# Latent attention: the softmax probabilities are normalised on ScalarE instead of VectorE

## The reference

```python
def blocked_attention(q, k, v, scale):
    ...
    def one_block(qblk):
        s = jnp.einsum('bqhgd,bkhd->bhgqk', qblk, k).astype(jnp.float32) * scale
        p = jax.nn.softmax(s, axis=-1).astype(v.dtype)
        return jnp.einsum('bhgqk,bkhd->bqhgd', p, v)
    ...

def mla_attend(q_nope, q_rope, ckv, k_rope, w_kv_b):
    B, T, _ = ckv.shape
    kv = (ckv @ w_kv_b).reshape(B, T, MLA_HEADS, QK_NOPE + V_DIM)
    k = jnp.concatenate([kv[..., :QK_NOPE],
                         jnp.broadcast_to(k_rope[:, :, None, :], (B, T, MLA_HEADS, QK_ROPE))], axis=-1)
    q = jnp.concatenate([q_nope, q_rope], axis=-1)[:, :, :, None]
    return blocked_attention(q, k, kv[..., QK_NOPE:], (QK_NOPE + QK_ROPE) ** -0.5)
```

## Time and profile before

| | us |
|---|---|
| median of 3 runs | 1293.79 (1293.59 to 1293.82) |
| the profiled execution, its own time | 1294.56 |
| its span, first to last instruction | 1292.7 |
| PE busy | 1262.9 (98% of the span) |
| DVE busy | 827.4 (64%) |
| ACT busy | 532.3 (41%) |
| latent-attention stage (first to last exponential of L1540) | 976.4 to 1155.3 |

### The profile page before, as it was taken

How to read it: one execution, slowest core, us unless ns; L and a number is a source line. 1 busy time by engine, 2 the same in 40 slices (tenths; PEclk the granted TensorE clock), 3 DMA queues, 4 the chain that set the end, 5 groups by cost and what they waited for, 6 DMA issues and landing times.

```text
span 1292.7 us, 17320 instructions
## 1 busy us (share of the span) xinstructions
PE 1262.9 (98%) x6691; PEld 1050.3 (81%) x6691; DVE 827.4 (64%) x1257; ACT 532.3 (41%) x967; POOL 58.2 (5%) x80
## 2 busy tenths in 40 slices
PE   5999999999999999999999999999999999999997
PEld 2556677788888878888887788999989999988885
DVE  3344756775667757675874767987386666664445
ACT  4234343354333333344334544333365554543333
POOL 0000300000100010000000200000000000000000
PEclk9999999999999999999999999999999999999999
DMA  9999788445666457644885467675332222226443
GB/s 388 399 417 392 281 303 284 141 145 178 222 217 228 126 191 238 203 159 155 284 297 168 146 216 242 213 240 170 120 99 79 68 65 66 66 65 247 154 151 134
DMA packets 65521, 257.17 MB, mean 199 GB/s; under 512 B 7992, under 2 KB 8120, under 8 KB 60320
## 3 DMA queue, kind: packets, MB, share of 16 engines
q1 hardware_dynamic: 59616, 234.96, 52.5%
q0 software_dynamic: 5536, 20.52, 4.9%
q10 hardware_dynamic: 288, 0.59, 0.1%
HBM read 248.10 MB, written 7.93 MB: 198 GB/s over the span
## 4 chain that ended last, share of the span: by engine, by line
PE 94%; DMA 2%; DVE 2%; issue 1%; ACT 1%; SPq 0%; POOL 0%; ACTq 0%; POOLq 0%
PE gemm L560 18%; PE gemm L562 17%; PE gemm L561 17%; PE turned L717 3%; PE gemm L758 3%; PE gemm L760 3%; PE gemm L759 3%; PE gemm L532 2%; PE gemm L534 2%; PE gemm L533 2%; PE attended L799 2%; PE ada_bank L696 2%; PE ada_bank L640 1%; DMA w_raw<-in_w_all 1%; PE scores L717 1%; DMA ada<-in_ada_first 1%
## 5 line engine op out<-in xcount | busy, mean ns | idle before, releaser
L1637 DVE TENSOR_TENSOR w_lo<-w_raw,w_hi 128x1024 fp32r<-128x1024 f32 x241 | 296.9, 1235 | 265.6 <-ACT w_hi L1161 265.1
L560 PE MATMUL gemm<-w_hi,act_lo 128*128 128x512 f32 x1002 | 401.9, 401 | 2.7 <-issue 1.2
L562 PE MATMUL gemm<-w_hi,act_hi 128*128 128x512 f32 x1002 | 391.4, 391 | 0.0
L561 PE MATMUL gemm<-w_lo,act_hi 128*128 128x512 f32 x1002 | 390.6, 390 | 0.0
L1161 ACT ACTIVATE w_hi<-w_raw 128x1024 fp32r<-128x1024 f32 x241 | 252.8, 1057 | 276.2 <-PE gemm L562 169.6
L560 PEld LDWEIGHTS gemm<-w_hi,act_lo 128*128 128x128 f32 x1002 | 188.4, 188 | 49.2 <-issue 12.1
L562 PEld LDWEIGHTS gemm<-w_hi,act_hi 128*128 128x128 f32 x1002 | 188.1, 188 | 40.6
L561 PEld LDWEIGHTS gemm<-w_lo,act_hi 128*128 128x128 f32 x1002 | 188.6, 188 | 36.6
L1735 DVE SCALAR_TENSOR_TENSOR ada<-ada,silu_c 128x1024 f32<-128x1024 f32 x62 | 76.9, 1277 | 0.0
L758 PE MATMUL gemm<-act_lo,w_hi 128*128 128x384 f32 x192 | 65.0, 338 | 0.0
L1735 DVE SCALAR_TENSOR_TENSOR gate_acc<-gate_ring,silu_c,gate_acc 128x1024 f32<-128x1024 f32 x52 | 64.3, 1278 | 0.0
(11 more groups left out here) (412 smaller groups left out, 1939.7 us busy)
## 6 DMA issues: line engine op xcount, KB each, us to landing
w_raw<-in_w_all SPq DMA_DIRECT2D x245, 512.0 KB, 3.7
ada<-in_ada_all SPq DMA_DIRECT2D x96, 512.0 KB, 5.5
ada<-in_ada_first SPq DMA_DIRECT2D x20, 1024.0 KB, 14.0
gate_ring<-in_ada_all SPq DMA_DIRECT2D x28, 512.0 KB, 4.4
ada_bias_room<-in_ada_first SPq DMA_DIRECT2D x6, 1024.0 KB, 14.6
ada_key_room<-in_ada_first SPq DMA_DIRECT2D x6, 1024.0 KB, 14.7
gate_bc<-gate_scratch POOLq DMA_DIRECT2D x4, 1024.0 KB, 6.6
st<-x_scratch POOLq DMA_DIRECT2D x4, 768.0 KB, 5.1
```

What stands on the lines that cost most here:

```text
L560: pe.matmul(bank_[:], alo, whi[:, kk], start=first, stop=False)
L561: pe.matmul(bank_[:], ahi, wlo[:, kk], start=False, stop=False)
L562: last = pe.matmul(bank_[:], ahi, whi[:, kk], start=False, stop=end)
L1637: dve.tensor_tensor(w_lo[:, r, 0:width], w_raw[:, r, 0:width], hi_slot(w)[:, 0:width].bitcast(F32), ALU.subtract).then_inc(lo_ready, 1)
```

## The change

The product with the reciprocal moves from VectorE to ScalarE. On VectorE `scale` becomes `invert`: the reciprocal alone, which raises the new semaphore `p_inverse`. On ScalarE a new function `normalise` waits for `p_inverse` and copies the probabilities onto themselves with the reciprocal as the per-partition scale; it raises `p_scaled`. It stands behind the exponential of its unit; for the first unit of a latent tile the high copy of `turned_p_high` stands between the two, and `normalise` of the first unit stands ahead of the exponential of the second.

```diff
+            def normalise(g, n):
+
+                at = g.n + n
+                part = prob[:, at % 3, 0:P if n < 2 else 3 * P]
+                act.wait_ge(p_inverse, at - N_UH + 1)
+                copy(part, part, rinv[:, at % 4:at % 4 + 1]).then_inc(p_scaled, 1)
...
                     if t > 0:
                         turned_p_high(g, n + 1)
                     if after is not None:
+                        normalise(after, m)
                         pair_exponent(after, m + 1)
+                        normalise(after, m + 1)
...
             for h in range(2):
                 pair_exponent(Pair(0), h)
+                normalise(Pair(0), h)
...
-            def scale(g, n):
+            def invert(g, n):
 
                 at = g.n + n
-                part = prob[:, at % 3, 0:P if n < 2 else 3 * P]
                 dve.wait_ge(p_ready, at + 1)
-                own.add(dve.reciprocal(rinv[:, at % 4:at % 4 + 1], rsum[:, at % 4:at % 4 + 1]))
-                own.sync()
-                dve.tensor_scalar(part, part, rinv[:, at % 4:at % 4 + 1], None, ALU.mult).then_inc(p_scaled, 1)
+                dve.reciprocal(rinv[:, at % 4:at % 4 + 1], rsum[:, at % 4:at % 4 + 1]).then_inc(p_inverse, 1)
...
                         for h in range(2):
                             maximum(after.n + m + h, (t + 1) % NT)
-                        scale(after, m)
+                        invert(after, m)
...
                     if after is not None:
-                        scale(after, m + 1)
+                        invert(after, m + 1)
```

More of the change, by code:

```diff
@@ L349, in build @@
         rope_ready = sem("rope_ready"); rope_hi = sem("rope_hi"); pair_low = sem("pair_low")
-        p_scaled = sem("p_scaled"); p_hi = sem("p_hi")
+        p_scaled = sem("p_scaled"); p_inverse = sem("p_inverse"); p_hi = sem("p_hi")
         o_made = sem("o_made"); o_gated = sem("o_gated"); o_hi = sem("o_hi"); o_low = sem("o_low")
@@ L2329, in _ @@
                 maximum(N_UH + h, 0)
-                scale(Pair(0), h)
+                invert(Pair(0), h)
             pair_attention(Pair(0), Pair(1))
```

## The result

| | before | after |
|---|---|---|
| median of 16 runs, us | 1293.79 (1292.93 to 1294.59) | 1296.52 (1295.66 to 1296.89) |
| ratio, 95% interval | | 1.0021 (1.0014 to 1.0028) |
| span of the profiled execution, us | 1292.7 | 1294.6 |
| VectorE busy, us | 827.4 | 812.6 |
| ScalarE busy, us | 532.3 | 554.0 |

The changed kernel is slower by 2.7 us (1.8 to 3.6). The forecast was 1296.4. The interval lies on both sides of 0.2%.

The account below looks back on a forecast made before the run. PE, busy for 98% of the span, was taken as the bound; -0.2 us at the start of pair 0 and +2.8 us in the last pair, added to the median 1293.79 us, gave 1296.4 us, range 1295.0 to 1298.4.

Parts of the forecast that it names:

- What bounds the kernel: Whole kernel: PE is busy 98% of the span, so only instants where PE waits or is spared a wait count.
- The price of a normalisation: ScalarE, each unit: 0.61 us for 384 columns (plain copy 0.515 plus 0.094 for the scale), 0.39 us for 128.
- cheaper normalisation: Rival, ScalarE copies: at 0.515 us each the change costs +2.1, 1295.9 us; at 0.421 us, 1295.4; chance 0.12.
- The round trip: ScalarE to VectorE and back: normalisation starts 0.91 us after its exponential; exponential, wait and normalisation hold ScalarE 1.42 us.
- Pairs with a successor: First seven pairs: ScalarE runs 0.59 us late, but unit 4's transpose has 0.3 us to spare; nothing added.
- the cover breaks in every pair: Rival: normalisations 0.15 us dearer make PE wait about 0.2 us in each of seven pairs; +4.4, 1298.2 us; chance 0.17.
- Pair 0: Start of the first pair: the second exponential no longer waits behind a scaling, PE's scores start 0.22 us earlier; -0.2 us.
- The last pair: Last pair, without cover: gated-head split +1.43 us, transpose of unit 4 +1.3, transpose of unit 5 +2.80.
- Not slower: Rival, last pair: VectorE, not ScalarE, sets it, so dropping four scalings gives -0.7, 1293.1 us; chance 0.11.
- The sum: Whole kernel: -0.2 + 2.8 = +2.6 us, added to the median 1293.79, gives 1296.4 us.
- same: Whole kernel: outcome within 0.2% (2.6 us) of the time before; chance 0.49.
- slower: Whole kernel: outcome beyond the 0.2% bound of 1296.4 us; chance 0.47.

Follow-up runs that it names:

- the second copy: Changed kernel plus an idle plain 256-column ScalarE copy behind the wait of each latent normalisation; 1300.92 us, 1.0054 against the kernel before.
- two other orders, on VectorE: Kernel before, with pair 0's maxima ahead of its scalings and the last pair's low part of values ahead of a gate; 1291.60 us, again 1292.24.

## Why the prediction held

- **What bounds the kernel.** Right: PE is 98% busy in both, and the whole difference lies at instants at which it waited or was spared a wait. Moving the last pair alone moved the whole loss.
- **The price of a normalisation.** 0.61 us predicted, 0.616 measured; 0.39 us for 128 columns, 0.40 measured. The scale operand was the right term to add (0.094 from the rows of before, 0.092 by experiment). Taking the plain copy would have given +2.1, the rival "cheaper normalisation"; it fell with the measured 0.616.
- **The round trip.** 0.91 us from an exponential to its normalisation predicted; 0.94 us in the last pair, where the reciprocal waited behind a maximum, and 0.88 us behind a normalisation.
- **Pairs with a successor.** Nothing predicted, nothing measured. The exponential of unit 4 was predicted 7.76 + 0.59 = 8.35 us after that of unit 2 and came after 8.32 (1050.97 and 1059.29). The low copy of unit 3 was to end 0.40 us before the weight load of unit 4's transpose and ended 0.43 us before it. I had taken 0.1 us off as what PE needs ahead of the load; the second copy says that this was 0.05 us too much for the normalisation of unit 4: it was to be ready 0.48 us before the load, was ready 0.51 us before it, and the measured cover is 0.48 us. The rival "the cover breaks in every pair" fell by this margin, and the second copy shows that it is a real one: 0.3 us more for each copy and it costs 3.4 us.
- **Pair 0.** -0.2 predicted, -0.27 in distance A. PE's wait for the exponential is gone: its scores start 0.02 us after the transpose ahead of them ends.
- **The last pair.** +1.43 at the split of a gated head (measured 2.87 - 1.45 = 1.42), +1.3 at the transpose of unit 4 (1.27), +2.80 at unit 5 (2.72). One sentence was wrong by carelessness: I gave 1.3 and 1.5 us as PE's idle time before units 4 and 5, and they are 1.51 and 1.32. The first has to include the 0.24 us that PE had waited there before. The second is the difference of the two delays (2.72 - 1.27 = 1.45 us) less 0.14 us: before, the transpose of unit 5 started at 1157.59, which is 0.14 us ahead of the modelled end of the matmul in front of it (1157.33 + 0.40), and the profile counts idle time from that end. The delays themselves, which make the sum, don't hang on this.

```profile
1157.33 0.40 PE L562 MATMUL gemm<-w_hi,act_hi 128*128 128x512 f32 x1
```

- **Not slower.** VectorE didn't set the last pair. It waited 2.00 us for the high copy of unit 4, which started 14.08 us after the first output matmul in place of 11.34.
- **The sum.** +2.6 predicted, +2.45 in the distances, +2.7 in the times. That the forecast lay on the 0.2% bound made the chances of "same" and "slower" nearly equal, and the measured interval, 1.0014 to 1.0028, doesn't settle which it was.

## What to carry to other kernels

When PE is the bound and the helpers have time to spare, don't price a moved step by the engine's load: lay it into the helper's list, and compare when each thing that PE waits for is ready with when PE asks. Look first at the place where the filler between two dependent steps is shortest, here the last pair: this exchange was free in seven rounds of eight and lost its whole price in the eighth. And look at what stands behind the new work on its engine; a third of this loss was an order (a split that nobody needed yet ahead of a copy that PE did). What made the kernel faster was two other orders, on VectorE, and no change of engine.

## What the runs showed of the hardware

- A ScalarE copy of 384 columns in place took 0.524 us with a constant scale and 0.616 us with a scale per partition, 0.092 us for the operand. For 128 columns it took 0.310 and 0.401 us, 0.091 us for it, so the price did not grow with the columns.
- A hand-over between ScalarE and VectorE cost 0.03 to 0.04 us: at pair 0 of the changed kernel the accumulator read ended at 976.33 and the reciprocal started at 976.36, and the copy followed its end by 0.04 us. The round trip is the durations of its instructions and little else (0.94 and 0.88 us in the last pair).
- The idle time that the profile prints before a matmul can be smaller than what there is to win, since it counts from the modelled end of the matmul before. The 0.27 us of pair 0 gave back 0.52 us (1.72 to 1.20 us from the first exponential to the scores) once nothing was waited for: the scores then started 0.02 us after the start of the transpose ahead of them, well before its modelled end, where before they had started 0.54 us after it (977.60 and 978.14). At the last pair, where some idle time was left, the two agreed: the printed wait fell by 0.87 us and A by 0.86. Distances between starts are the better measure.
